# Native float32 matmuls with the expert weights stationary, in a mixture-of-experts step

## What is computed

```python
def expert_choice_moe(h, w_router, w_gate, w_up, w_down):
    B, L, D = h.shape
    cap = max(1, EC_CAPACITY_FACTOR * L // N_EXPERTS)
    aff = jax.nn.softmax(jnp.einsum('bld,de->ble', h, w_router).astype(jnp.float32), axis=-1)
    gate, idx = lax.top_k(jnp.swapaxes(aff, 1, 2), cap)
    xs = jax.vmap(lambda hb, ib: hb[ib])(h, idx)
    hid = jax.nn.silu(jnp.einsum('becd,edf->becf', xs, w_gate)) * jnp.einsum('becd,edf->becf', xs, w_up)
    out = jnp.einsum('becf,efd->becd', hid, w_down) * gate[..., None].astype(h.dtype)
    return jax.vmap(lambda ob, ib: jnp.zeros((L, D), ob.dtype).at[ib.reshape(-1)].add(ob.reshape(-1, D)))(out, idx)
```

## Time and profile before

| | us |
|---|---|
| median of 3 runs | 2321.33 |
| the three runs | 2320.47 to 2323.99 |
| span of the profiled execution | 2323.6 |
| trunk and router, up to the first matmul of expert 0 | 717.0 |
| the 16 experts, 717.0 to the end of the last matmul | 1578.3 |
| tail behind the last matmul | 28.2 |

### The profile page before, as it was taken

The page is one execution under the profiler, slowest core; times in us unless marked ns, Lnnn a source line. Parts: engine busy times, 40 slices in busy tenths (PEclk is TensorE's granted clock), DMA queues, the critical chain, the costliest instruction groups (busy, mean ns, idle before and its releaser), DMA issues.

```text
span 2323.6 us, 38034 instructions
## 1 busy us (share of the span) xinstructions
PE 2171.7 (93%) x15246; PEld 2032.3 (87%) x15246; DVE 1606.1 (69%) x1306; ACT 1319.9 (57%) x1052; POOL 227.6 (10%) x242
## 2 busy tenths in 40 slices
PE   6899999999966999999999999999999999999994
PEld 2898689999956999899999999999999998999994
DVE  0534642232466887888888888888888888788884
ACT  3333443213134676766767667676676766667673
POOL 1212205301110000000000000000000000000000
PEclk9999999999977999999999999999999999999997
DMA  8223542222455999999999999999999999999993
GB/s 272 67 74 115 176 146 73 91 73 74 164 205 183 345 365 345 369 353 352 370 346 363 360 360 365 344 367 344 370 358 344 372 340 370 354 353 367 354 369 127
DMA packets 515877, 646.91 MB, mean 278 GB/s; under 512 B 8700, under 2 KB 506600, under 8 KB 515816
## 3 DMA queue, kind: packets, MB, share of 16 engines
q1 hardware_dynamic: 507376, 617.72, 77.7%
q0 software_dynamic: 8320, 28.27, 4.0%
q10 hardware_dynamic: 120, 0.04, 0.0%
HBM read 631.79 MB, written 14.20 MB: 278 GB/s over the span
## 4 chain that ended last, share of the span: by engine, by line
PE 81%; issue 9%; DVE 4%; ACT 3%; DMA 2%; POOL 0%; DVEq 0%; SPq 0%; ACTq 0%; POOLq 0%
PE bank L1330 57%; PE bank L1571 18%; PE bank L1304 2%; ACT we_hi L827 2%; PE bank L1378 1%; DVE we_lo L1174 1%; DMA raw_t<-in_w_ada_dram 1%; DVE hid L1245 1%; PE bank L1437 1%; DVE wt_lo L901 0%; ACT wt_hi L651 0%; DMA x_rows<-h_scratch,idx_gather 0%; PE bank L1448 0%; DVE h_tmp L988 0%; PE bank L1506 0%
## 5 line engine op out<-in xcount | busy, mean ns | idle before, releaser
L1174 DVE TENSOR_TENSOR we_lo<-raw_e,we_hi 128x2816 fp32r<-128x2816 f32 x384 | 1186.2, 3089 | 243.9 <-ACT we_hi L827 242.0
L827 ACT ACTIVATE we_hi<-raw_e 128x2816 fp32r<-128x2816 f32 x384 | 980.9, 2559 | 248.3 <-PE bank L1571 151.4
L1330 PE MATMUL bank<-we_hi,xs_hi 128*80 128x352 f32 x2048 | 666.6, 325 | 1.1 <-DVE xs_lo L1223 1.1
L1330 PE MATMUL bank<-we_hi,xs_lo 128*80 128x352 f32 x2048 | 659.9, 322 | 0.0
L1330 PE MATMUL bank<-we_lo,xs_hi 128*80 128x352 f32 x2048 | 659.8, 322 | 0.0
L1571 PE MATMUL bank<-we_hi,hd_hi 128*80 128x256 f32 x1408 | 404.3, 287 | 33.9 <-DVE hd_lo L1223 33.9
L1571 PE MATMUL bank<-we_hi,hd_lo 128*80 128x256 f32 x1408 | 402.5, 286 | 0.0
L1571 PE MATMUL bank<-we_lo,hd_hi 128*80 128x256 f32 x1408 | 401.8, 285 | 0.0
L1330 PEld LDWEIGHTS bank<-we_lo,xs_hi 128*80 128x80 f32 x2048 | 304.1, 148 | 25.2
L1330 PEld LDWEIGHTS bank<-we_hi,xs_hi 128*80 128x80 f32 x2048 | 303.7, 148 | 24.5 <-ACT small L856 1.4
L1330 PEld LDWEIGHTS bank<-we_hi,xs_lo 128*80 128x80 f32 x2048 | 304.4, 149 | 22.3
(11 more groups left out here) (248 smaller groups left out, 2344.4 us busy)
## 6 DMA issues: line engine op xcount, KB each, us to landing
raw_e<-in_w_exp_gate_dram SPq DMA_DIRECT2D x128, 1408.0 KB, 9.2
raw_e<-in_w_exp_up_dram SPq DMA_DIRECT2D x128, 1408.0 KB, 8.4
raw_e<-in_w_exp_down_dram SPq DMA_DIRECT2D x128, 1408.0 KB, 9.4
raw_t<-in_w_ada_dram SPq DMA_DIRECT2D x24, 1024.0 KB, 5.2
raw_t<-in_w_in_dram SPq DMA_DIRECT2D x14, 1024.0 KB, 4.9
raw_t<-in_w_branch_gate_dram SPq DMA_DIRECT2D x8, 1024.0 KB, 5.4
raw_t<-in_w_ret_out_dram SPq DMA_DIRECT2D x4, 1024.0 KB, 5.1
raw_t<-in_w_out_dram SPq DMA_DIRECT2D x4, 1024.0 KB, 5.1
```

Of the source, the lines that this page charges most:

```text
L827: nc.scalar.activation(we_hi[n % SPLIT_E][:], raw_e[:, n % RAW_E, :], ACT.Copy).then_inc(e_hi, 1)
L1174: nc.vector.tensor_tensor(we_lo[n % SPLIT_E][:], raw_e[:, n % RAW_E, :], we_hi[n % SPLIT_E][:].bitcast(F32), ALU.subtract).then_inc(e_lo, 1)
L1330: ins = mm(out, a, b, start=i == 0, stop=i == count - 1)
```

## The change

- `ring` is one store of 12 slots (`SLOTS`) of 11 264 bytes per partition. Gate and up come in 16 blocks of 128 whole rows of 2816 numbers; down in 8 blocks of two or three times 128 rows of 1024 numbers. Slots 0 to 3, 4 to 7 and 8 to 11 are filled for the first time when their memory is free of the trunk's data (`e_free`).
- The split of the weights and of the activations is gone: no `we_hi`, `we_lo`, `xs_lo`, `hd_hi`, `hd_lo`, and no work of ACT and DVE on them.
- PE multiplies plain float32. The stationary operand is a 128 x 128 piece of the weights, the moving operand is the activation, 80 columns. An expert has 2 x 8 x 22 = 352 matmuls for gate and up and 22 x 8 = 176 for down, 528 in all.
- Gate and up sums stay open in all eight banks for eight blocks each; hidden values come out with the hidden dimension in the partitions, so the 22 transposes of `hid` are gone. The output comes out transposed: ACT and DVE copy it to `out_t`, and PE transposes it in 8 pieces, behind the second block of the next expert.
- The first expert is written out as well; the loop has 14 passes.

```diff
-RAW_E = 6
-SPLIT_E = 3
+GROUP = (0, 6, 12, 18, 22)
+SLOTS = 12
+DOWN_AT, DOWN_N = (0, 3, 6, 9), (3, 3, 3, 2)
...
-                    sp.wait_ge(e_lo, e * NB + n + 1)
+                    if n < SLOTS and n % 4 == 0:
+                        sp.wait_ge(e_free[n // 4], 1)
+                    sp.wait_ge(e_used, e * NB + n + 1 + (1 if n >= 16 and n % 4 < 3 else 0))
...
-            def e_split(e, n):
-                dve.wait_ge(e_hi, e * NB + n + 1)
-                nc.vector.tensor_tensor(we_lo[n % SPLIT_E][:], raw_e[:, n % RAW_E, :],
-                                        we_hi[n % SPLIT_E][:].bitcast(F32), ALU.subtract).then_inc(e_lo, 1)
...
+            def hidden(e, n, first):
+
+                k, up = n % KT, n // KT
+                landed(e, n)
+                w = slot(n)
+                for t in range(FT):
+                    g = t // 6
+                    if k == 0 and t == 12 and not first:
+                        if not up:
+                            pe.wait_ge(e_osb["act"], e)
+                            pe.wait_ge(e_osb["dve"], e)
+                        else:
+                            pe.wait_ge(e_out, 2 * e)
+                    o = bank[4 * up + g][:, (t - GROUP[g]) * CAP:(t - GROUP[g] + 1) * CAP]
+                    ins = mm(o, w[:, t * P:(t + 1) * P], x_t[:, k, :], start=k == 0 and t == GROUP[g], stop=k == KT - 1,
+                             skip_group_check=True)
+                    if k == KT - 1 and t + 1 == GROUP[g + 1] and g < NG - 1:
+                        ins.then_inc(e_ufull if up else e_gfull, 1)
+                ins.then_inc(e_used, 1)
...
+            def down(e, n):
...
+                    if t in GROUP:
+                        pe.wait_ge(e_hid, NG * e + GROUP.index(t) + 1)
+                    for j in range(KT):
+                        o = bank[2 + j // 4][:, j % 4 * CAP:(j % 4 + 1) * CAP]
+                        ins = mm(o, w[:, i, j * P:(j + 1) * P], hid_t[:, t, :], start=t == 0 and j % 4 == 0, stop=t == FT - 1,
+                                 skip_group_check=True)
...
+            def expert(e, first, last):
+                pe.wait_ge(e_x, 2 * e + 2)
+                for n in range(2 * KT):
+                    hidden(e, n, first)
+                    if n == 1 and not first:
+                        out_transpose()
+                pe.wait_ge(e_silu, NG * e + NG)
+                for n in range(2 * KT, NB):
+                    down(e, n)
+                    if n == 18 and not last:
+                        x_transpose(e + 1)
```

More of the change, by code:

```diff
@@ L291, in build @@
[L291 to L298, removed]
+        sh2_b = [at("sh2_sample", dead + 26400, [P, D]), at("sh2_prompt", dead, [P, D])]
@@ new lines, in _ @@
+            x_to_t(0)
+            def expert(e, last):
+                for g in range(NG):
+                    n = GROUP[g + 1] - GROUP[g]
+                    if g < NG - 1:
+                        act.wait_ge(e_gfull, 3 * e + g + 1)
+                    else:
+                        act.wait_ge(e_used, SLOTS + NB * e + 8)
+                    nc.scalar.activation(silu_g[:, GROUP[g]:GROUP[g + 1], :],
+                                         bank[g][:, 0:n * CAP].rearrange("p (a b) -> p a b", a=n), ACT.Silu).then_inc(e_silu, 1)
+                if not last:
+                    x_to_t(e + 1)
+                act.wait_ge(e_used, SLOTS + NB * e + NB)
+                nc.scalar.activation(out_t[:, 4:8, :], bank[3][:, 0:4 * CAP].rearrange("p (a b) -> p a b", a=4), ACT.Copy)\
+                  .then_inc(e_osb["act"], 1)
@@ L1271, in _ @@
+                dve.wait_ge(s_idx, e + 3)
+                for i in range(2):
+                    dve.wait_ge(e_outt, 2 * e + i + 1)
+                    nc.vector.scalar_tensor_tensor(
+                        out=out_rows[:, i * 512:(i + 1) * 512], in0=bank[6 + i][0:CAP, :], scalar=gate_cur[:, 0:1],
+                        in1=g2_rows[:, i * 512:(i + 1) * 512], op0=ALU.mult, op1=ALU.mult).then_inc(e_out, 1)
             with dve.Fori(0, NE - 1) as e:
@@ L1521, in _ @@
             transpose(tr(("ga", 0, 0))[0:CAP, 0:NE], top_v[:]).then_inc(tr_full, 1)
-            def group(e, g):
-                if g >= NJ:
-                    pe.wait_ge(e_gath, 16 * e + 32)
-                else:
-                    pe.wait_ge(e_hid, NJ * e + NJ + g + 1)
-                if not (isinstance(e, int) and e < 0):
-                    pe.wait_ge(e_tr_split, NG * e + NG + g - 1)
-                n = 4 if g >= NJ else TILE_EDGE[g % 4 + 1] - TILE_EDGE[g % 4]
-                for i in range(n):
-                    t = 4 * (g - NJ) + i if g >= NJ else TILE_EDGE[g % 4] + i
-                    src = (x_rows if g >= NJ else hid)[:, t * P:(t + 1) * P]
-                    ins = transpose(bank[5 + g % 2][:, i * CAP:(i + 1) * CAP], src)
-                ins.then_inc(e_tr, NJ + 1 if isinstance(e, int) and e < 0 and g == NJ else 1)
@@ L1578, in _, with x_transpose @@
-            with pe.Fori(0, NE - 1) as e:
-                expert(e, False)
-            expert(NE - 1, True)
-DOWN_BANK = (4, 7)
-TR_AFTER = {**{2 * g + 2: g for g in range(NJ)}, 2 * NJ + 3: NJ, 2 * NJ + 4: NJ + 1}
+            def x_transpose(e):
+                pe.wait_ge(e_gath, 16 * e + 16)
+                for i in range(2):
+                    for a in range(4):
+                        k = 4 * i + a
+                        ins = transpose(bank[i][:, a * CAP:(a + 1) * CAP], x_rows[:, k * P:(k + 1) * P])
+                    ins.then_inc(e_xt, 1)
@@ L1586 @@
+            x_transpose(0)
+            expert(0, True, False)
+            with pe.Fori(1, NE - 1) as e:
+                expert(e, False, False)
+            expert(NE - 1, False, True)
+            pe.wait_ge(e_osb["act"], NE)
+            pe.wait_ge(e_osb["dve"], NE)
+            out_transpose()
 N_CONST = 6
```

251 lines of the change are left out of this document (90 added, 161 removed).

## The result

The changed kernel takes 3243.6 us in the median of four executions (3241.2 to 3341.1), the kernel before took 2322.0 beside it. The ratio is 1.396, with a 95% interval of 1.394 to 1.398: 922 us slower, where 318 were forecast. The longest of the four ran at a mean clock of 0.78 instead of 0.81 and is left out of the ratio. The profiled execution has a span of 3241.9 us. The table puts the stages beside the forecast (first matmul and tail by order of time).

A forecast was written before the change was run, and what follows sets the result against it. PE was taken as the bound, with weight loads setting the new pace: 707 + 16 x 117.2 + 15 x 1.9 + 30 = 2641 us, stated as 2640, 318 us or 14% slower; range 2585 to 2780.

The forecast's parts named there:

- The pace of the pairs: Expert matmuls on PE: each load-and-matmul pair takes 0.111 us (0.107 to 0.120), set by the weight load; 1056 pairs an expert.
- The expert at the full clock: One expert on PE: 117.2 us of pairs plus 1.9 us of transposes and changes between transposes and matmuls.
- The router and the tail: Ahead of and behind the experts: first matmul at 707 instead of 717 us; tail 30 instead of 28.2 us.
- The covered waits: Waits the change adds at down's start, bank 2, the x_rows copies, gather and scatter: all hidden, costed at nothing.
- The ring: Weight transfers: an expert's 34.6 MB take 87 to 99 us, under 119, so the ring stays full.
- The roles in turn: Rival for PE's pairs: a 128-column load can't run beside a matmul, 172 ns a pair, 3670 us in all; chance 2%.
- the first rival: PE's loop no longer stays on the chip, each branch back waits for a fetch: 53 to 125 us, 2693 to 2765; 25%.
- the first forecast: Expert loop on PE: bound by weight loads, with instruction fetches hidden, 2640 us; chance 65%.
- The price of the fetch: At each branch back of PE's loop: priced like a small gather under load, 3.8 to 8.9 us, 14 passes.
- The clock: Rival: PE streaming columns for 65 of 111 ns loses its full clock, 0.21 us a pair, some 4300 us; chance 3%.

The follow-up runs named there:

- the first two experiments: The changed kernel with PE's loop branch announced early, 2779.5 us; then the same plus six unread 512-column matmuls ahead of expert 0, 2658.6 us.
- its long pass: The kernel before with PE's loop over two experts in a pass, 2712 loads and matmuls, same work: 2354.0 us, ratio 1.013.
- the first experiment: The changed kernel with PE's loop branch back announced ahead of time, so that the code at the pass's head is fetched early: 2779.5 us, ratio 1.196.
- the change with early fetch and dense matmuls: The changed kernel with the announced branch back and six unread float32 matmuls of 512 moving columns ahead of expert 0: 2658.6 us, ratio 1.144.

## Why the forecast missed

**Right.** *The pace of the pairs*: 0.111 us was taken, 0.112 measured, and both halves of the argument hold in their own experiments: fewer moving columns change nothing, fewer stationary ones bring it to 0.07. *The expert at the full clock*: 119.1 forecast, 119.3 measured. *The router and the tail*: 707 and 30, measured 707.4 and 30.3. *The covered waits*: no wait for `ring`, `hid_t`, or the copy to `out_t` in the list of PE's waits. *The ring*: DMA at some 290 GB/s at the full clock, about the 300 of the forecast. *The roles in turn* (3670) can be dropped, 0.112 being far from 0.172. And the observation that q8's packets with PE's issue waits once in a pass would mean the first rival was the one that held.

**Wrong: the choice between the first forecast and the rival "the loop no longer stays on the chip".** The trace of before had shown the row that told it: 1356 loads and matmuls to a pass, not one packet on q8, and 2144 in the new one. It had 25%. What spoke against it, that matmuls already issued may cover a short fetch, would fit the low clock alone, where the waits are 1.0 to 1.8 us; at the full clock they are 4.2 to 4.8. There are 13 of them, not 14. The price of the fetch was sized well: 3.8 to 8.9 us, measured at the lower end.

**Wrong: the term for what a wait costs.** This is the step that failed. The prediction had the wait and the clock as two rivals, each with its own price (53 to 125 us, and about 1700), and added nothing for one leading to the other. In "The clock" it said that PE never idles longer than it does now. By its own first rival PE would idle 3.8 to 8.9 us in each pass, twice the 2.1 of the earlier trace rows, so that sentence and that rival couldn't both be kept. Had they been joined, the term would have been (wait + low stretch x 0.476) for each branch. What the runs show in its place: 48 us of waits and 429 us of low clock behind them. The trace of before held the sign. The prediction put the 4.4 us that its sum of an expert lacked down to the transposes and what lies around them; 1.5 of them are the low clock behind a wait of 2.1 us.

**Wrong: the router's end.** The forecast took the first matmul 10 us earlier and priced all behind it at the full clock. The earlier trace rows say that the clock is low at that point; before, it is back within 4 us of the first matmul. With the new stream it stayed low for 249 us, 118 of the missing 601. The prediction used the low clock of rows 13 only as an estimate of the worst case; it did not ask what, in the new stream, would end it.

Both come from one omission: it was asked whether the new stream would lose the clock, not whether it would win it back.

**Open.** Every low stretch of the change, and those behind the late waits of the first two experiments, ended 1.4 to 4.3 us after the start of the eight transposes of `out_t`, a short run in which each load is 80 columns long and each matmul 128. But the same eight passed without effect some 19 us into each of the three long stretches, and there it took the next expert's. The eight transposes of `x_rows` never ended one, nor did any in the run with 40 moving columns. Why they sometimes do and sometimes don't was not settled, nor why 2 of the 16 short waits of before, and one of 2.8 us in its long pass, left the clock alone, and no run was made that moves or adds such transposes alone. That one of four executions of the first experiment took 103 us more would fit its last wait meeting the second kind: from 2635 us to the last matmul the work takes 112 us at the full clock and 102 more at the low one. That execution was not profiled, nor was the one of the change that took 98 us more than its others, so this is only argued. How many moving columns between 40 and 80 keep the clock was not tried either.

## What to carry over

Where the trace shows that a stage depends on PE's clock, price a wait as the wait plus the low stretch behind it, and ask what in the following stream brings the clock back: here it was a few microseconds where the matmuls were longer than their loads, and up to 252 where the loads set the pace. Count the instructions of a loop's pass before and after an edit, and compare them with a pass that the trace shows to be kept. And when weights become the stationary operand of narrow products, make the sum for the loads: with 128 stationary and 80 moving columns they set the pace, not the products.

## What the runs showed of the hardware

- The clock has a memory in this sense: the same instructions at the same PE busy share (no gap in 1640 us of the first experiment, one of 1.8 us in 1340 to 1580 us of the change) ran at 1.00 in one and 0.50 in the other, depending on what came before. The Trainium skill ("TensorE: Matmul & The Clock Gate", What's actually happening) says that the throttled state is the default and that activity releases it; the change's 249 us behind the router show a stream that PE executes without pause and that releases nothing until 956 us.
- A wait of 1.9 us between loads (the change with early fetch and dense matmuls) already lowered the clock, and so did those of 2.1 us of the kernel before, in 14 of 16 cases.
- With 80 moving columns the clock came back 3 to 6 us after PE resumed where a load had 64 columns, and 20 to 252 us after it where it had 128.
- A branch back to code that isn't kept makes PE wait 4.2 to 4.9 us at the full clock in the kernels of the change (2.8 to 4.4 with the old matmuls), with 120 packets of 16 KB in 1900 us, about 150 KB a pass. With the loop's back edge hinted, the packets remain and the wait is gone where DMA's share is 0.82; at 1.01 waits of 3.5 to 4.0 us were there all the same.
- Longer pieces load faster: 407 GB/s for whole rows (half of the stationary columns), against 398 and 348 for the pieces of before.
